# A two-layer streaming encoder: whole program unrolled, S5 matrices made by VectorE in the first feed-forward, S5 steps pipelined behind w_in

## What is computed

```
layer 0: h += mla(rmsnorm(h));  h += conv_ffn(rmsnorm(h))
layer 1: h += s5(rmsnorm(h));   h += conv_ffn(rmsnorm(h))
out = rmsnorm(h)

conv_ffn(h): up = h @ w_up                    # 1024 -> 2 * 2816
             up = causal depthwise conv of 3 taps over tokens, + bias
             val, gate = split(up);  return (silu(gate) * val) @ w_down

s5(h): u = h @ w_in, as 64 groups of 16 channels
       x[s] = a * x[s-1] + Bbar u[s]          # 64 complex states a group
       y = Re(C x) + D u;  y = gelu(y)
       val, gate = split(y @ w_glu);  return val * sigmoid(gate)
```

## Time and profile before

| | |
|---|---|
| median of 3 runs | 1348.83 us (1344.48 to 1350.65) |
| span of the profiled execution | 1348.3 us, and its time the same |
| PE busy | 1248.7 us (93%) |
| DVE busy | 791.1 us (59%) |
| ACT busy | 469.7 us (35%) |
| POOL busy | 272.0 us (20%) |
| mean granted TensorE clock | 0.92 of full |

### The profile page before, as it was taken

One profiled execution on the slowest core, in us unless ns is written; L12 is line 12 of the kernel. 1 busy time (PEld: TensorE's weight loads), 2 busy tenths in 40 slices (PEclk: granted clock), 3 DMA queues, 4 the chain that ended last, 5 costly groups with the idle time before them and its releaser, 6 DMA issues.

```text
span 1348.3 us, 16700 instructions
## 1 busy us (share of the span) xinstructions
PE 1248.7 (93%) x5468; PEld 1006.8 (75%) x5468; DVE 791.1 (59%) x1108; ACT 469.7 (35%) x635; POOL 272.0 (20%) x321
## 2 busy tenths in 40 slices
PE   5998999997799999999899988899999999999996
PEld 3776578776587878878678877678777788878874
DVE  6677545678657753766644554255466537753665
ACT  5414534563123432444111111143366324432442
POOL 4730002899884000000422330000000000000000
PEclk9999999998899999999866665689999999999998
DMA  4221014232343333222423332233222322223322
GB/s 160 71 94 48 1 32 151 85 92 62 125 140 106 96 94 94 93 78 91 137 82 102 108 99 68 62 94 93 78 94 93 93 95 93 93 94 96 97 80 86
DMA packets 64829, 123.09 MB, mean 91 GB/s; under 512 B 23696, under 2 KB 34192, under 8 KB 64784
## 3 DMA queue, kind: packets, MB, share of 16 engines
q1 hardware_dynamic: 63632, 118.35, 28.1%
q0 software_dynamic: 1152, 4.19, 0.8%
HBM read 111.05 MB, written 11.47 MB: 91 GB/s over the span
## 4 chain that ended last, share of the span: by engine, by line
PE 64%; DVE 19%; ACT 6%; issue 5%; DVEq 3%; DMA 1%; SPq 1%; ACTq 0%
PE bank L1178 17%; PE bank L1179 17%; PE bank L1180 17%; DVE WL L636 4%; PE bank L1379 3%; PE bank L1381 3%; PE bank L1383 2%; DVE CV L847 2%; ACT WH L422 2%; DVE AL L832 2%; ACT CV L549 1%; DVE Z L841 1%; DVE HH L828 1%; DVE MX L765 1%; PE bank L1356 1%
## 5 line engine op out<-in xcount | busy, mean ns | idle before, releaser
L636 DVE TENSOR_TENSOR WL<-RAW,WH 128x1024 fp32r<-128x1024 f32 (+1 forms) x184 | 236.3, 1284 | 216.4 <-ACT WH L422 212.6
L1178 PE MATMUL bank<-GH,WH 128*128 128x512 f32 x816 | 330.9, 405 | 34.6 <-DVE Z L841 17.6
L1179 PE MATMUL bank<-GL,WH 128*128 128x512 f32 x816 | 323.2, 396 | 0.0
L1180 PE MATMUL bank<-GH,WL 128*128 128x512 f32 x816 | 322.9, 396 | 0.0
L422 ACT ACTIVATE WH<-RAW 128x1024 fp32r<-128x1024 f32 (+1 forms) x184 | 190.1, 1033 | 351.8 <-PE bank L1180 272.9
L1178 PE MATMUL bank<-AH,WH 128*128 128x512 f32 x596 | 241.6, 405 | 20.5 <-DVE AL L832 10.6
L1179 PE MATMUL bank<-AL,WH 128*128 128x512 f32 x596 | 236.9, 397 | 0.0
L1180 PE MATMUL bank<-AH,WL 128*128 128x512 f32 x596 | 236.3, 396 | 0.0
L1178 PEld LDWEIGHTS bank<-GH,WH 128*128 128x128 f32 x816 | 156.8, 192 | 79.6 <-DVE Z L841 25.8
L1179 PEld LDWEIGHTS bank<-GL,WH 128*128 128x128 f32 x816 | 157.3, 193 | 32.7 <-issue 1.2
L1180 PEld LDWEIGHTS bank<-GH,WL 128*128 128x128 f32 x816 | 156.4, 192 | 33.8
(11 more groups left out here) (230 smaller groups left out, 1316.4 us busy)
## 6 DMA issues: line engine op xcount, KB each, us to landing
RAW<-in_w_up SPq DMA_DIRECT2D x88, 512.0 KB, 3.5
RAW<-in_w_dn SPq DMA_DIRECT2D x32, 512.0 KB, 3.5
RAW<-in_w_glu SPq DMA_DIRECT2D x16, 512.0 KB, 3.5
RAW<-in_w_dn SPq DMA_DIRECT2D x16, 384.0 KB, 3.0
RAW<-in_w_wo SPq DMA_DIRECT2D x8, 512.0 KB, 3.6
od_scratch<-OO POOLq DMA_DIRECT2D x8, 512.0 KB, 3.1
RAW<-in_w_win SPq DMA_DIRECT2D x8, 512.0 KB, 3.5
OO<-od_scratch SPq DMA_DIRECT2D x8, 512.0 KB, 3.4
```

What stands on the lines that cost most here:

```text
L636: v.tensor_tensor(WL[p][:, :n], RAW[p][:, :n], WH[p][:, :n].bitcast(F32), ALU.subtract).then_inc(s_lo, 1)
L1178: mm(out, wh, hi_[:, k, :], start=start, stop=False)
L1179: mm(out, wh, lo_[:, k, :], start=False, stop=False)
L1180: return mm(out, wl, hi_[:, k, :], start=False, stop=stop)
```

## The change

- **Unrolled.** No engine has a loop any more; `pair_loop` and `s5_loop` go. WH and WL have 3 buffers (RH = 3), RAW stays at 2. Blocks of the feed-forwards, w_o and w_glu rotate over three banks, those of the first attention phase over four. In an up block VectorE reads the bank first and makes WL three blocks ahead after it; ACT makes WH three blocks ahead.
- **S5 matrices.** For each j VectorE does twelve operations of 128x512 (`matrix_op`), 96 in all, one in each up block and three in each down block of the first feed-forward (`OPS_AT`), with 8 of 12 reading the powers in steps of 128 bytes. TensorE's `matrices(j)` stands where `MAT_AT` puts it: j = 0 at up00 block 13, 1 at dn00 4, 2 at up01 2, 3 at up01 9, 4 at dn01 3, 5 at dn01 7, 6 at up02 5, 7 at dn02 3. ACT copies ET, which is kept for all eight j, and the lags. OO, GM, TA and TB have one buffer each; GpSimd's DMAs `spill` and `lags` carry OO and the lags to DRAM.
- **GpSimd.** Powers, CIN, BBR and BBI are made during the attention. WC and WS follow once every block before dn00 is done, and after them come spill(j) and lags(j) for all j.
- **S5 stage.** Three pieces run as a pipeline behind w_in: block t of w_in, inputs(t-2), outputs(t-3) on TensorE; u_out(t), states(t-2), y_lo(t-4) on VectorE. Each transposing transfer is one DMA. `states` works on 128x512 at once. The decay table RT is made by ACT.

The diff, cut to what is spoken of:

```diff
+def _bank(b):
+    n = PHASE_OF[b]
+    i = b - FIRST[n]
+    if n == "wa":
+        return (0, 1, 6, 7)[i % 4]
+    if n == "win":
+        return i % 2
+    if n == "glu":
+        return i % 3
+    if n in ("uq", "uk", "uv"):
+        return i % 2
+    return (0, 1, 7)[(b - FIRST["wo" if b < FIRST["win"] else "up10"]) % 3]
+BANK = [_bank(b) for b in range(NBLOCKS)]
...
+def bank_free(b):
+    if PHASE_OF[b] in ("uq", "uk", "uv"):
+        return b - 1
+    return max([c + 1 for c in range(b) if BANK[c] == BANK[b]], default=0)
...
+OPS_AT = {}
+_i = 0
+for _b in FFN0:
+    _n = 1 if PHASE_OF[_b].startswith("up") else 3
+    OPS_AT[_b] = range(_i, min(_i + _n, MAT_OPS * NJ))
+    _i = OPS_AT[_b].stop
+assert _i == MAT_OPS * NJ
+MAT_AT = {}
+for _b in FFN0:
+    for _i in OPS_AT[_b]:
+        if _i % MAT_OPS == MAT_OPS - 1:
+            _n = _b + 2
+            while _n - FIRST[PHASE_OF[_n]] < 2:
+                _n += 1
+            MAT_AT[_n] = _i // MAT_OPS
+assert len(MAT_AT) == NJ and max(MAT_AT) + 1 < FIRST["win"]
...
+            def matrix_op(i):
+                j, o = divmod(i, MAT_OPS)
+                sh = [P, QJ, C, LQ]
+                qs = slice(QJ * j, QJ * j + QJ)
+                if o < 6:
+                    pr, pi = (t[:, 1:LQ + 1, qs] for t in (PWR, PWI))
+                    cr, ci = CRE, CIN
+                else:
+                    pr, pi = (t[:, LQ - 1::-1, qs] for t in (PWR, PWI))
+                    cr, ci = BBR, BBI
+                pr, pi = (x.rearrange("p m q -> p q m").unsqueeze(2).broadcast_to(sh) for x in (pr, pi))
+                cr, ci = (x[:, qs, :].unsqueeze(3).broadcast_to(sh) for x in (cr, ci))
+                if i == 0:
+                    dve.wait_ge(s_pw, 2)
+                if o % 3 == 0:
+                    v.drain()
+                if o == 0:
+                    v.tensor_tensor(TA[:], pr, cr, ALU.mult)
+                elif o == 1:
+                    v.tensor_tensor(TB[:], pi, ci, ALU.mult)
+                elif o == 2:
+                    v.drain()
+                    if j >= 1:
+                        dve.wait_ge(s_et, j)
+                        dve.wait_ge(s_ow, 16 * j)
+                    v.tensor_tensor(OO[:, 0], TA[:], TB[:], ALU.add)
...
+                            v.tensor_tensor(Z[p][:, 2:S + 2], bank[BANK[b]][:], RSTD[:], ALU.mult).then_inc(s_ev, 1)
+                            last = i == n - 1 and p == 1
+                            if not last:
+                                lo(b + RH)
...
+                            if last:
+                                lo(b + RH)
+                            else:
+                                matrices_of(b)
...
+            for t in range(NJ + 4):
+                if t < NJ:
+                    u_out(t)
+                if 2 <= t < NJ + 2:
+                    states(t - 2)
+                if t >= 4:
+                    y_lo(t - 4)
...
+            g.tensor_scalar(CIN[:], CIN[:], -1.0, None, ALU.mult)
+            cmul(BBR[:], BBI[:], f["cr"].unsqueeze(2).broadcast_to([P, NQ, C]),
+                 f["ci"].unsqueeze(2).broadcast_to([P, NQ, C]), BRE[:], BIM[:], BBT[:, 0], BBT[:, 1]).then_inc(s_pw, 1)
+            pool.wait_ge(s_mm, FIRST["dn00"])
             g.memset(WC[:, :, 0:1], 1.0)
             g.memset(WS[:, :, 0:1], 0.0)
             g.drain()
             n = 1
             wk = ((f["wr"], f["wi"]), (f["k"], f["th"]))
...
+            m.then_inc(s_wcs, 1)
+            def spill(j):
                 pool.wait_ge(s_O, j + 1)
...
+                g.dma_start(OD[j], OO[:].rearrange("p r q c s -> p r (q c s)")).then_inc(s_ow, 16)
+            def lags(j):
+                pool.wait_ge(s_kt, j + 1)
+                g.dma_start(KD_[j], KT[:]).then_inc(s_kw, 16)
+            for j in range(NJ):
+                spill(j)
+                lags(j)
...
+            def matrices(j):
+                pe.wait_ge(s_bbk, j + 1)
+                pe.wait_ge(s_O, j + 1)
+                pe.wait_ge(s_G, j + 1)
+                if j >= 1:
+                    pe.wait_ge(s_etc, j)
+                    pe.wait_ge(s_k0, j + 1)
+                for r in range(2):
+                    for q in range(QJ):
+                        mm(bank[6][32 * q:32 * q + 32, 0:P], BBK[:, r, q, :], OO[:, r, q].rearrange("p c s -> p (c s)"),
+                           start=(r == 0), stop=(r == 1), skip_group_check=True)
+                for r, t in enumerate((CRE, CIN)):
+                    for q in range(QJ):
+                        mm(bank[2][32 * q:32 * q + 32, 0:C], BBK[:, r, q, :], t[:, QJ * j + q, :],
+                           start=(r == 0), stop=(r == 1), skip_group_check=True)
+                for r in range(2):
+                    for q in range(QJ):
+                        m = nc.tensor.transpose(bank[4 + r][:, q * P:(q + 1) * P],
+                                                GM[:, r, q].rearrange("p c s -> p (c s)"), IDENT[:])
+                m.then_inc(s_et, 1)
...
+            def inputs(j):
+                pe.wait_ge(s_ur[j % 3], 16 * (j // 3 + 1))
+                if j == 0:
+                    pe.wait_ge(s_etc, NJ)
...
+            def outputs(j):
+                p = j % 2
+                pe.wait_ge(s_tmr[p], 16 * (j // 2 + 1))
+                if j >= 2:
+                    pe.wait_ge(s_g, j - 1)
+                for gi in range(2):
+                    for q in range(QJ):
+                        mm(bank[4 + 2 * p + gi][:, q * NK:(q + 1) * NK], TM[p][:, 2 * q + gi, :], U2[j % 3][:, 2 * q + gi, :],
+                           start=(q == 0), stop=False, skip_group_check=True)
+                pe.wait_ge(s_X, j + 1)
+                pe.wait_ge(s_or[p], 16 * (j // 2 + 1))
+                for r, x in enumerate((XR, XI)):
+                    for q in range(QJ):
+                        for gi in range(2):
+                            rows = slice(64 * gi, 64 * gi + 64)
+                            m = mm(bank[4 + 2 * p + gi][:, q * NK:(q + 1) * NK], O2[p][rows, r, q, :], x[p][rows, q, 0:NK],
+                                   start=False, stop=(r == 1), skip_group_check=True)
+                m.then_inc(s_Y, 1)
...
-            for j in range(7, 11):
-                s5_step(j // 2, j % 2)
-            glu_steps(range(4, KD - 1))
-            glu_steps([KD - 1])
-            other_pairs("glu", KD, AH, AL)
+            for t in range(2, NJ):
+                whole(FIRST["win"] + t, KD, GH, GL)
+                inputs(t - 2)
+                if t >= 3:
+                    outputs(t - 3)
+            inputs(NJ - 2)
+            outputs(NJ - 3)
+            inputs(NJ - 1)
+            outputs(NJ - 2)
+            glu_part((0, 1), range(0, 4))
+            outputs(NJ - 1)
+            glu_part((0, 1), (4, 5))
+            glu_part((2,), range(0, 6))
+            glu_part((0, 1, 2), (6,))
```

More of the change, by code:

```diff
@@ L87 @@
 WIDTH = {"q": Q_LORA, "kv": KV_LORA}
[L90 to L123 removed]
+FFN0 = range(FIRST["up00"], FIRST["win"])
+MAT_OPS = 12
+OPS_AT = {}
[14 more added lines that the diff above has]
+assert len(MAT_AT) == NJ and max(MAT_AT) + 1 < FIRST["win"]
 def build(nc, d):
@@ L405, in _ @@
+            for b in range(FIRST["win"] + 4 + NJ, NBLOCKS):
+                load(b)
             for k in range(KD):
@@ L613, in glu @@
+            for i in range(KD):
+                b = FIRST["glu"] + 2 * i + 1
                 for p in range(2):
-                    b = FIRST["glu"] + 2 * i + p
-                    act.wait_ge(s_mm, b + 1)
-                    hi_next("glu", i, p, last)
-                if not (isinstance(i, int) and i == 0):
+                    act.wait_ge(s_mm, b + p)
+                    hi(b - 1 + p + RH)
+                if i > 0:
                     act.wait_ge(s_ev, b - 1)
-                act_(SIG[:], bank[1][:], ACT.Sigmoid).then_inc(s_sig, 1)
@@ L1152, in inputs @@
-            def inputs(j):
-                pw, ch, a, b_ = views(j)
-                if not (isinstance(j, int) and j == 0):
-                    pool.wait_ge(s_et, j)
-                cmul(GR[:], GI[:], pw(PWR, 0), pw(PWI, 0), ch(BBR), ch(BBI), a, b_, s_G)
-            for j in range(2):
-                outputs(j, j)
-            with pool.Fori(1, 4) as i:
-                for p in range(2):
-                    outputs(2 * i + p, p)
-            for p in range(2):
-                pool.wait_ge(s_ow[p], 16 * 4)
@@ new lines, in ffn @@
+            def ffn(l, norm, tile0):
+                for t, (f0_, n) in enumerate(THIRDS):
+                    up, dn = f"up{l}{t}", f"dn{l}{t}"
+                    first_pair(up, tile0, KD, GH, GL, norm=norm if t == 0 else None)
+                    for b in span(up)[2:]:
+                        if b in MAT_AT:
+                            matrices(MAT_AT[b])
+                        whole(b, KD, GH, GL)
+                    first_pair(dn, TILE0[f"h{l}{t}"], n, AH, AL, ahead=n // 2)
+                    for b in span(dn)[2:]:
+                        if b in MAT_AT:
```

(2 more changed lines are left out.)

1036 lines of the change are left out of this document (451 added, 585 removed).

## The result

The changed kernel takes 1238.8 us (median of 4 runs, 1237.37 to 1241.98) against 1347.4 us for the kernel before in the same measurement: a ratio of 0.9195, 95% interval 0.9175 to 0.9216. The forecast was 1284 with a range of 1248 to 1316. It falls on the number of rival (a), 1237, but as will be seen not for the reason of that rival.

What follows compares the result with a forecast made beforehand. No single bound: a serial S5 step at low clock, and a TensorE-bound first feed-forward slowed by GpSimd and table loads. -107 + 52 - 4 - 3 = -62 from 1348.8 gives 1286.8, stated as 1284; range 1248 to 1316.

Steps and rivals of the forecast that it cites:

- rival (a): First feed-forward: VectorE's operation 14, waiting for GpSimd's first spill, costs little; 1237 us, chance 0.08.
- part 1: S5 stage: a pipeline of shorter steps, with the matrices moved out, saves 107 us (87 to about 120).
- I take 16, between the two: S5 stage: a step takes 16 us, between 14.0 with row halves side by side and 18.0 without overlap.
- the 14.0 us that it took for the lower end: S5 stage: step time if two row halves run side by side, outputs falling from 7.6 to 5.3 us at full clock.
- Half clock: S5 step: without overlap, half the outputs take 6.6 us at half clock; tokens cost about 1 us more than 5.44.
- The wait for the spill: First feed-forward: VectorE's operation 14 waits for GpSimd's first spill behind WC and WS; +47 us, between +36 and +67.
- part 2: First feed-forward: goes from 399.2 to 451 us, +52 (+25 to +72).
- Matrix operations: First feed-forward: strided products on VectorE take 1.07 us, plain sums 0.68, adding 2.1 us a pair of up blocks.
- 22 pairs lose 0.7 each: +16: First feed-forward up blocks: VectorE needs 11.6 us a pair against TensorE's 10.88, costing 16 us.
- Matrices on TensorE and j = 3: First feed-forward: matrices take about 2.6 us, three of eight cost, +8; VectorE's wait for j = 2's transposes, +10.
- the second row of the table: First feed-forward in the stage comparison: 399.2 us before, 442.9 after, +43.7 against +52 forecast.
- The second feed-forward: Second feed-forward: a pair takes 11.51 us against 10.88, six such pairs with the loop's table loads gone: -4 us.

Runs made afterwards that it cites:

- grouped halves: Changed kernel with XR and XI issued for all tiles of row half 0, then of row half 1, instead of alternating halves: 1247.1 us, ratio 0.9251.

## Why the prediction was wrong

**The S5 step (part 1): mis-sized, and the cause of the miss.** Failed are the sentence "I take 16, between the two" and the 14.0 us that it took for the lower end. The measured step is 10.61. The terms: tokens 6.5 forecast, 5.67 measured; inputs 1.1, as measured; outputs 8 or so with the clock falling in them, 3.86 measured. For outputs the prediction allowed one gain, two row halves side by side, and priced it at 0.30 a triple; it left TM at 0.36. That gain is real: the halves start together, which is worth 1.8 us an output. But both prices were taken from the old triple, and each held a change of height, 0.14 us; the new order has 14 changes fewer, 2.0 us an output, and that term the prediction put at nothing. So outputs at full clock are 3.86 and not 5.3. With outputs short the second effect followed: small matmuls last 4.9 us a step, and the clock stays at 2.4 GHz, so neither outputs nor tokens pay for half of it. Taken back to the old order, the step is 17.4 us and the kernel 67 us slower, so order and clock together hold the miss. Over the stage the steps give about 25 of the 36 us (the outputs behind token block 7 end at 741.75, 61.3 us after UB(0) at 680.4, forecast 86.7), the tail the rest.

The rule of the Trainium skill that a change of the tiling mode drains the engine ("TensorEngine Tiling (Array Packing)", Key Properties) was weighed for the new order's disadvantage. The old order changes the height of its products 15 times in an output, the new one once. By that rule the new order gains, and the runs agree in sign: each change costs 0.14 us. The page gives no price, and no run shows whether it is a drain. The changes could have been counted in the code, and the prediction did not count them.

**Half clock.** Right for the old order (the step of 17.4 us above), wrong for the new, where it fell only behind the last token block. Between token blocks the clock stayed at 2.4 GHz with 4.9 us of small matmuls in the changed kernel and fell in some steps with 5.5 (grouped halves). In the old order, whose small matmuls would last 8.7 us at full clock and lasted 10.0, it fell in all four steps that were looked at.

**The wait for the spill (part 2): right.** Forecast 47 us, TensorE idle 47.48. The chain was sized 43 and took 44.1. (The 47.48 are idle time alone; the pair with this wait is 50.3 us longer than one of 10.88, since TensorE comes back at half clock, 0.51 from 372.6 to 378 us.) What the prediction did not say is what removing it would bring: 30 us only, 45 with the matrices placed anew, since TensorE then waits more for the matrices, 21.9 us in place of 9.1.

**Matrix operations: right in price, wrong in where they cost.** The price is 1.10 us, forecast 1.07. The sum "22 pairs lose 0.7 each: +16" failed: the pairs of up blocks, counted from the starts of their matmuls, take 10.88 us in the changed kernel wherever they hold no matrices and no turn of the thirds. That VectorE needs more than TensorE's pace shows later, as TensorE's waits in front of matrices and hidden tiles. Leaving out 56 of the 64 strided products gave 8 to 11 us back, so the size is near the forecast, but by another way than forecast.

**Matrices on TensorE and j = 3.** The wait of VectorE was sized 10 and is 9.17, but costs TensorE nothing at its place; TensorE stands 4.47 us at the matrices of j = 3 and 2.48 at the last. Matrices take 299.52 to 301.05, 1.5 us and not 2.6, but a pair with matrices that waits for nothing takes 12.63 against 10.88, 1.75 more, and all eight stand in TensorE's way, not three: by that 14 us where 8 were forecast. So the 8 us of the second row of the table are 16 that the pairs did not lose, less 6 more for the matrices and some 3 more around the wait for the spill; the 9.1 us of waits in front of matrices stand where 10 were forecast.

**The second feed-forward.** The table loads of the weight copy are gone (13 at L422 before, 1 now). Of the 8.3 us the pairs give 4, as forecast. The rest is at the first pair of each down phase: 12.92, 11.75 and 13.77 us before, 10.88, 10.88 and 11.99 now. No run tells the deeper ring of weight halves from the missing loop. It isn't the third bank: with two banks these pairs take 10.88, 10.88 and 11.96.

**Rival (a)** met the number by chance: it said that the wait would cost little, and the wait cost 47 us. Right number, wrong cause.

## What to carry to other kernels

When small matmuls of different heights are interleaved, count how often the height changes before pricing them by the mean of a triple, sort them by height, and let the two row halves alternate: 24 products in another order, in each of eight outputs, gave 43 us of 1347 in the old kernel. Where a step's small matmuls decide its clock, price both branches whole (here 10.6 and 17.4 us) and not a value between them, since a shorter stretch of small matmuls gains twice, by its own length and by the clock. A single buffer that one queue empties ties its refill to everything ahead in that queue; when it is untied, look where the next engine is late.
